# Strassen's algorithm for 18 up-projection tile pairs, with the weight sums on GpSimd

## What is computed

```python
def swiglu(x, w1, w3, w2):
    return (jax.nn.silu(x @ w1) * (x @ w3)) @ w2
...
    x = x + 0.5 * rmsnorm(swiglu(rmsnorm(x, norm_g[0]), ffn1_w1, ffn1_w3, ffn1_w2), norm_g[1])
    mo, st = mixer(rmsnorm(x, norm_g[2]), w_in, ...)
    x = x + rmsnorm(mo, norm_g[3])
    x = x + 0.5 * rmsnorm(swiglu(rmsnorm(x, norm_g[4]), ffn2_w1, ffn2_w3, ffn2_w2), norm_g[5])
```

## Time and profile before

| | us |
|---|---|
| median of 3 runs | 1088.48 |
| range of the runs | 1088.02 to 1089.86 |
| span of the profiled execution | 1087.4 |
| PE busy in it | 1077.2 (99%) |
| VectorE busy | 533.9 (49%) |
| ScalarE busy | 358.4 (33%) |
| GpSimd busy | 95.5 (9%) |

### The profile page before, as it was taken

How to read it: one execution, slowest core, us unless ns; L and a number is a source line. 1 busy time by engine, 2 the same in 40 slices (tenths; PEclk the granted TensorE clock), 3 DMA queues, 4 the chain that set the end, 5 groups by cost and what they waited for, 6 DMA issues and landing times.

```text
span 1087.4 us, 21585 instructions
## 1 busy us (share of the span) xinstructions
PE 1077.2 (99%) x8945; PEld 1063.8 (98%) x8945; DVE 533.9 (49%) x929; ACT 358.4 (33%) x527; POOL 95.5 (9%) x169
## 2 busy tenths in 40 slices
PE   8999999999999999999999999999999999999998
PEld 8999999999999999998999999999999999999997
DVE  6444524343333369685656787743323343324346
ACT  5322114222122345321537543532212222122232
POOL 0000725920000000340000000000000000000000
PEclk9999999999999999999999999999999999999999
DMA  7223232222222241123421134132222222222232
GB/s 253 83 78 96 80 94 81 93 83 91 82 88 82 78 136 40 60 78 122 135 62 59 60 117 148 40 98 95 80 94 80 94 83 91 85 90 89 76 88 83
DMA packets 30338, 99.13 MB, mean 91 GB/s; under 512 B 3652, under 2 KB 6084, under 8 KB 30152
## 3 DMA queue, kind: packets, MB, share of 16 engines
q1 hardware_dynamic: 30280, 98.33, 28.7%
HBM read 93.58 MB, written 4.74 MB: 90 GB/s over the span
## 4 chain that ended last, share of the span: by engine, by line
PE 95%; DVE 2%; ACT 1%; issue 1%; DMA 0%; SPq 0%; DVEq 0%; ACTq 0%
PE ps L2013 77%; PE ps L2038 6%; PE ps L2107 3%; PE ps L2481 2%; PE ps L2125 1%; PE ps L2045 1%; PE ps L2050 1%; PE ps L2305 0%; PE ps L2264 0%; DMA x<-xT 0%; PE ps L2255 0%; PE ps L2331 0%; DVE wl L1019 0%; PE ps L2298 0%; PE ps L2272 0%
## 5 line engine op out<-in xcount | busy, mean ns | idle before, releaser
L1019 DVE TENSOR_TENSOR wl<-raw,wh 128x1024 fp32r<-128x1024 f32 (+1 forms) x145 | 178.1, 1229 | 409.2 <-ACT wh L563 408.6
L2013 PE MATMUL ps<-xh,wh 128*128 128x272 f32 x1616 | 336.3, 289 | 1.2 <-DVE k L1437 1.0
L2013 PE MATMUL ps<-xl,wh 128*128 128x272 f32 x1616 | 333.7, 288 | 0.0
L2013 PE MATMUL ps<-xh,wl 128*128 128x272 f32 x1616 | 332.8, 287 | 0.0
L563 ACT CAST wh<-raw 128x1024 fp32r<-128x1024 f32 (+1 forms) x145 | 150.6, 1038 | 422.4 <-PE ps L2013 419.6
L2013 PEld LDWEIGHTS ps<-xh,wh 128*128 128x128 f32 x1616 | 253.0, 188 | 2.5 <-issue 1.4
L2013 PEld LDWEIGHTS ps<-xl,wh 128*128 128x128 f32 x1616 | 254.1, 189 | 0.0
L2013 PEld LDWEIGHTS ps<-xh,wl 128*128 128x128 f32 x1616 | 252.9, 188 | 0.0
L2013 PE MATMUL ps<-hh,wh 128*128 128x272 f32 x608 | 126.3, 289 | 0.5 <-DVE hl L1040 0.5
L2013 PE MATMUL ps<-hl,wh 128*128 128x272 f32 x608 | 125.4, 287 | 0.0
L2013 PE MATMUL ps<-hh,wl 128*128 128x272 f32 x608 | 125.3, 287 | 0.0
(11 more groups left out here) (483 smaller groups left out, 1181.9 us busy)
## 6 DMA issues: line engine op xcount, KB each, us to landing
raw<-w SPq DMA_DIRECT2D x118, 512.0 KB, 3.5
raw<-win SPq DMA_DIRECT2D x25, 512.0 KB, 3.5
raw<-w SPq DMA_DIRECT2D x16, 384.0 KB, 3.1
raw<-wout SPq DMA_DIRECT2D x8, 512.0 KB, 3.6
o_yT<-x SPq DMA_DIRECT2D x8, 272.0 KB, 2.2
cs<-cT SPq DMA_DIRECT2D x4, 516.0 KB, 4.4
o_sC<-cs SPq DMA_DIRECT2D x4, 516.0 KB, 6.4
x<-xT SPq DMA_DIRECT2D x3, 544.0 KB, 6.8
```

The source lines that it names most:

```text
L1019: V.tensor_tensor(wl[par][:, 0:cols], raw[par][:, 0:cols], wh[par][:, 0:cols].bitcast(F32), ALU.subtract).then_inc(split_done, 1)
L2013: last = mm(ps[:, bank + s, 0:HALF], w[:, kk * P:(kk + 1) * P], a[:, kk, s * HALF:(s + 1) * HALF], start=(kk == 0 and i == 0), stop=(kk == ...
```

## The change

18 of the 22 tile pairs (a gate tile and its up tile) of the second FFN are computed by Strassen's algorithm, in its form with seven products: the 2x2 blocks of the weights are K halves by gate and up tile (A11, A12, A21, A22), those of x are K halves by token halves. A product has 4 K tiles x 3 passes = 12 matmuls of 128x272. The four weight sums of a pair (S1 and S3 in one instruction of 1024 elements, S2 and S4 with 512 each) are made by GpSimd. The weight blocks and sums are then cast by ScalarE and get their low parts from VectorE; partial results are copied out of PSUM by ScalarE (`keep_p1`, `keep_p5`, `keep_u2`) and added in PSUM by VectorE (`c11`, `c12`, `c22`). The parts become 4, 6, 6 and 6 tiles; the first four pairs are computed as before, and a part more of eight down units comes about, with the same number of matmuls in all.

The products need a normed x. VectorE writes it (`xn`, eight instructions), GpSimd makes the four sums of its blocks (`form_t3`, `form_t24`), and ScalarE and VectorE split those and three blocks. All this stands in part 0. The results of the first four pairs are brought to the same norm by one more multiplication each (`scaled`). Loads of the pairs have buffers of their own (`pair0`, `pair1`, 1 MB a pair); the sums lie where the two `raw` buffers were.

```diff
-assert sum(PARTS) == FT
+PARTS2 = (4, 6, 6, 6)
+assert sum(PARTS) == FT and sum(PARTS2) == FT and PARTS2[-1] == PARTS[-1]
+NG = sum(PARTS2[1:])
+KH = KD // 2
+KHP = KH * P
+FORM = KH * HALF
...
+FFN2_END = FFN2_BASE + 2 * PARTS2[0] + KD * (len(PARTS2) - 1)
+EARLY_STORES = 4 + MH
...
+        pairs = [sb(f"pair{i}", [P, 4 * KHP], at=er_at + 16 * KHP * i) for i in range(2)]
+        sums = sb("sums", [P, 4 * KHP], at=raw_at)
...
+            def load_pair(j):
+                if j == 0:
+                    spe.wait_ge(out_dma, 16 * EARLY_STORES)
+                elif j == 1:
+                    spe.wait_ge(form_lo, 1)
+                else:
+                    spe.wait_ge(a22_lo, j - 1)
+                    spe.wait_ge(s4_sum, j - 1)
+                tile = 2 * (PARTS2[0] + j)
+                for c in range(2):
+                    spe.dma_start(pairs[j % 2][:, c * UNIT:(c + 1) * UNIT], A["w13_1"][tile + 1 - c]).then_inc(pair_in[j % 2], 16)
...
+                load_pair(0)
+                load_pair(1)
...
+            def hi_g(j):
+                pair_full(j)
+                if j % N6:
+                    act.wait_ge(p1_done, j)
...
+                    act.wait_ge(unit_used, down_unit(j // N6, KD - 2) + 3)
...
+            def hi_form(i, dst, src, scale):
+                act.wait_ge(form_raw, i + 1)
+                if i == 0:
+                    act.wait_ge(unit_used, FFN2_BASE + 5)
+                    act.wait_ge(out_dma, 16 * EARLY_STORES)
+                nc.scalar.activation(dst, src, ACT.Copy, scale=scale).then_inc(form_hi, 1)
...
+                silu(hb + 2, 0)
+                hi_form(0, form_hi_t[:, 2], form_t3[:], 1.0)
+                hi_form(1, form_hi_t[:, 0], xn[:, 0, 1], 1.0)
+                hi_form(2, form_hi_t[:, 1], form_t24[:], -1.0)
+                hi_form(3, form_hi_t[:, 3], form_t24[:], 1.0)
+                up_split(u0 + 7)
+                hidden_hi(hb + 2, 0, 2)
...
+                            hi_4(j)
+                            hi_a22(j)
+                            if j > j0:
+                                silu_pair(j - 1)
+                            keep_p1(j)
+                            if last:
+                                act.wait_ge(p1_done, j + 1)
+                                down(0)
+                            else:
+                                hi_g(j + 1)
+                            keep_p5(j)
+                            keep_u2(j)
+                            if last:
+                                act.wait_ge(p6_done, j + 1)
+                                down(1)
+                            else:
+                                hi_3(j + 1)
+                                hi_12(j + 1)
+                            if j > j0:
+                                hidden_hi(FT4 + j - 1, 0, j - 1 - j0)
...
+            def low(hi, j, dst, src, rounded, done):
+                dve.wait_ge(hi, j + 1)
+                V.tensor_tensor(dst, src, rounded.bitcast(F32), ALU.subtract).then_inc(done, 1)
...
+            def c22(j):
+                dve.wait_ge(p7_done, j + 1)
+                dve.wait_ge(p5_kept, j + 1)
+                a, d = bank_a(j), set_of(j) + 3
+                V.tensor_tensor(ps[:, d, 0:HALF], ps[:, a, 0:HALF], p5_keep(j), ALU.add).then_inc(c22_done, 1)
...
+                for kk in range(KD):
+                    normed(kk)
+                up_lo(u0 + 6)
+                up_first(hb + 2, 0, u0 + 4)
+                lo_form(0, form_lo_t[2][:], form_t3[:], form_hi_t[:, 2], 1.0)
+                lo_form(1, form_lo_t[0][:], xn[:, 0, 1], form_hi_t[:, 0], 1.0)
+                lo_form(2, form_lo_t[1][:], form_t24[:], form_hi_t[:, 1], -1.0)
+                scaled(hb + 2, 0)
+                lo_form(3, form_lo_t[3][:], form_t24[:], form_hi_t[:, 3], 1.0)
+                up_lo(u0 + 7)
+                gated(hb + 2, 0, u0 + 5)
+                hidden_lo(hb + 2, 0, 2)
...
+                            if j > j0:
+                                c12(j - 1)
+                            lo_4(j)
+                            lo_a22(j)
+                            c11(j)
+                            if last:
+                                down(0)
+                            else:
+                                lo_g(j + 1)
+                            if j > j0:
+                                c22(j - 1)
+                            if last:
+                                down(1)
+                            else:
+                                lo_3(j + 1)
+                                lo_12(j + 1)
+                            if j > j0:
+                                hidden(j - 1)
+                                hidden_lo(FT4 + j - 1, 0, j - 1 - j0)
...
+            pool.wait_ge(xn_ready, KD)
+            pool.wait_ge(out_dma, 16 * EARLY_STORES)
+            G.tensor_tensor(form_t3[:], xn[:, 1, 1], xn[:, 0, 1], ALU.subtract).then_inc(form_raw, 1)
+            pool.wait_ge(form_raw, 1)
+            G.tensor_tensor(xn[:, 0, 1], xn[:, 0, 0], xn[:, 0, 1], ALU.subtract).then_inc(form_raw, 1)
+            pool.wait_ge(form_raw, 2)
+            G.tensor_tensor(form_t24[:], xn[:, 0, 1], xn[:, 1, 1], ALU.add).then_inc(form_raw, 1)
+            pool.wait_ge(form_lo, 3)
+            G.tensor_tensor(form_t24[:], form_t24[:], xn[:, 1, 0], ALU.subtract).then_inc(form_raw, 1)
+            for j in range(NG):
+                w = pairs[j % 2]
+                pool.wait_ge(pair_in[j % 2], 32 * (j // 2 + 1))
+                if j % N6:
+                    pool.wait_ge(s12_lo, j)
+                    pool.wait_ge(s3_lo, j)
+                else:
+                    pool.wait_ge(split_done, down_unit(j // N6, KD - 1) + 3)
+                if j:
+                    pool.wait_ge(s4_sum, j)
+                G.tensor_tensor(two(sums[:, 2 * KHP:]), two(w[:, KHP:3 * KHP]),
+                                w[:, A21B].unsqueeze(1).to_broadcast([P, 2, KHP]), ALU.add).then_inc(s13_sum, 1)
+                pool.wait_ge(s13_sum, j + 1)
+                G.tensor_tensor(sums[:, S2B], sums[:, S1B], w[:, A11B], ALU.add).then_inc(s2_sum, 1)
+                if j:
+                    pool.wait_ge(s4_lo, j)
+                pool.wait_ge(s2_sum, j + 1)
+                G.tensor_tensor(sums[:, S4B], sums[:, S2B], w[:, A12B], ALU.add).then_inc(s4_sum, 1)
...
+            def product(w, at, form, bank, first, done=None):
+                (w_hi, w_lo), (f_hi, f_lo) = w, form
+                for kk in range(KH):
+                    cut = slice(at + kk * P, at + (kk + 1) * P)
+                    for i, (a, f) in enumerate(((w_hi, f_hi), (w_hi, f_lo), (w_lo, f_hi))):
+                        ins = mm(ps[:, bank, 0:HALF], a[:, cut], f[:, kk], start=(first and kk == 0 and i == 0),
+                                 stop=(kk == KH - 1 and i == 2), skip_group_check=True)
+                if done is not None:
+                    ins.then_inc(done, 1)
...
+            def p4(j):
+                pe.wait_ge(a22_lo, j + 1)
+                pe.wait_ge(c22_done, j + 1)
+                product(a22_w[j % 2], 0, form_x[3], bank_a(j), False, p4_done)
...
+                            p2(j)
+                            p1(j)
+                            if j > j0:
+                                p7(j - 1)
+                            p5(j)
+                            p6(j)
+                            if j > j0:
+                                p4(j - 1)
+                            p3(j)
+                        p7(j)
+                        enter_down(0)
+                        down(0, range(0, 3))
+                        p4(j)
+                        down(0, range(3, n - 1))
+                        enter_down(1)
+                        down(1, range(0, n - 1))
+                        down(0, range(n - 1, n))
+                        down(1, range(n - 1, n))
...
-                if b == 1:
+                if b > 0:
```

348 lines of the change are left out of this document (339 added, 9 removed).

## The result

| | before | after |
|---|---|---|
| median of the runs, us | 1089.06 (1088.02 to 1089.86, 4 runs) | 1104.41 (1101.29 to 1107.65, 4 runs) |
| ratio, 95% interval | | 1.0139 [1.0116, 1.0162] |
| span of the profiled execution, us | 1087.4 | 1105.8 |
| mean granted clock of that span | 1.000 | 0.988 |
| first matmul of the mixer's last entry unit to first half unit of FFN 2, us | 364.7 | 382.4 |

The kernel became slower by 15.3 us (1.4%). The forecast was 7.3 us slower, so the direction was right and the size was half of what came. The last row of the table is the stretch in which everything that changed lies. It grew by 17.7 us in the profiled executions (after's is the slowest of its four runs, 1107.65); ahead of it the unchanged code came 0.9 us later by chance, and the tail behind it stayed the same (32.0 us before, 31.8 after).

The account below looks back on a forecast made before the run. PE's matmuls were taken to bound the kernel: 27.1 us removed, 33.2 us of waits added where 0.5 were before, net +5.6, plus 1.7 for the clock and 1.1 from span to median, gave 1095.8 us from 1087.4; range 1081.0 to 1106.0.

Parts of the forecast that it names:

- Removed work: 18 tile pairs of the second FFN: 84 matmuls each instead of 96, 27.1 us less.
- (a): Unit 6 of part 0: PE waits 2.2 us for its low part, behind VectorE's writing of xn.
- (f): Inside the parts: c22 comes 0.8 us late in two of each part's pairs, as GpSimd holds VectorE; 4.7 us.
- (b): Unit 7: PE waits 11.5 us for its low part, behind four low parts of forms and GpSimd's sums.
- (c): Down unit 2 of part 0: waits 1.6 us for y's first evacuation, and 0.1 before it.
- (d): Down unit 2 of parts 1 to 3: weights free late, then cast and low part; 1.95 each, 5.9 us.
- (e): First and second pairs of a part: products wait for [A11 A12] and sums; 2.2 and 5.0 us.
- Exclusion in one lane: In the pairs: VectorE instructions with two SBUF inputs and GpSimd sums exclude each other, filling 9.7 of 10.5 us.
- (g): Granted clock after PE's 11 us stand at unit 7: 1.7 us lost, at least nothing, at most twice that.
- The lane costs little: Rival for the pairs: GpSimd's sums let VectorE in or run some 20% faster; 1082.6 us, chance 0.20.
- The lane overflows: Rival for the pairs: longer sums or slower loads, c22 late in nearly every pair; 1103 us, chance 0.15.
- The prologue alone: Rival for part 0: the wait at unit 7 is shorter, 1088 +- 1, no change; near nothing, chance 0.10.

Follow-up runs that it names:

- e10_all_vector: After with activation blocks spread out, second pair's load moved, down unit 0 finished early, c22 placed earlier, pairs' weight sums on VectorE; 1075.27 us, 0.9867 of before.
- e3_small_sums: After with GpSimd's weight sums cut to 8 columns, casts and low parts reading raw blocks; 1089.57 us.
- e5_free_sums: After with GpSimd's weight sums at full size, but casts and low parts reading raw blocks and no cast waiting for a sum; 1102.67 us.
- e11_all_gpsimd: After with blocks spread out, load moved, down unit 0 finished early, c22 earlier, weight sums left on GpSimd; 1081.34 us, 0.9916 of before.
- e1_fill: After with filler matmuls, whose results nobody reads, put on TensorE ahead of nine of its waits; 1099.72 us.
- e9_prologue3: After with the seven activation blocks spread out and the second pair's load queued behind down unit 3's; 1092.82 us.
- e12_stands: The kernel before with five TensorE stands of some 2.0 us put into its second FFN; 1103.56 us, 1.0124 of before.

## Why the prediction was right in direction and half in size

- **Removed work, 27.1 us.** Right. It comes out once the waits go: e10_all_vector's stretch is 14.8 us shorter than before's, with 8.8 us of holes of 0.4 us and more and one short fall of the clock (1.6 us) in it; the other 1.9 are in gaps too small to be told apart.
- **Waits (a) to (f), 33.2 us.** Right place by place, 35.2 us in all: (a) 2.42 against 2.2, (b) 11.41 against 11.5, (c) 1.74 against 1.7, (d) 6.2 against 5.9, (e) 7.9 against 7.2, (f) 5.5 against 4.7. All but (b) are a little longer than laid out, 2.0 us together.
- **Exclusion in one lane.** Right, and shown by e3_small_sums against e5_free_sums. The lengths taken from two short rows held: 2.4 us for 1024 columns where 2.37 was taken. The reason given for (f), that c22 is late because the lane is full, was only half of it: c22 had a better place free, and with it e11_all_gpsimd has no such wait under the same sums.
- **(g) The clock, 1.7 us, 3.4 at most.** This is the step that failed. It asked only what a stand of 11 us costs and took the cold start for it; unit 7 then took 8.16 us instead of 6.02, 2.1 us, within its bounds. But the layout itself held seven more stands of 2 us, and the step gave them nothing, without a reason. Four of them were followed by a fall, 1.6 us each. In the profiled executions the clock cost 8.0 us (the stretch of e1_fill against after's) to 9.6 (with the 1.6 us that e1_fill's filler ran over its stands), so some 7 us more than forecast. Over the medians it is 4.7 to 6.3, so 3 to 4.6 more. Together with the 2.0 us of longer waits that is 5.0 to 6.6 of the 8.6 us between 1095.8 and 1104.4. The kernel before was itself 0.6 us slower beside after than in the runs the forecast started from. Some 1.4 to 3 us of the medians remain open. The profiled executions close better: holes 35.2, clock 2.1 + 4 x 1.6 = 8.5, less 27.1, are 16.6 of the 17.7 us by which the stretch grew, and the rest is of the size of e10_all_vector's small gaps.
- **The rivals.** "The lane costs little" fell on the means of 1978 and 1360 ns. "The lane overflows" gave 1103 and was nearest in time, but for a cause that isn't there: c22 is late in seven places, not in nearly all, and from the second pair of a part on the pairs start 10.6 to 11.6 us apart, with 12.1 only in the two where the clock fell. "The prologue alone" fell with (b), which measured 11.41 us.
- **What would show it.** The single wait of 9 to 12 us near 720 to 732, the clock below 1.00 behind it, the raised means and the waits on L1438 all came. The sign that would have shown the failed step, falls of the clock elsewhere, was not on the list.
- **Small slips in the sums.** The ten durations of VectorE's pair add up to 7.2 us, and to 6.4 with the overlap that is named beside them, not to 7.1; 6 x 0.8 in (f) is 4.8, not 4.7. Neither moves the forecast by more than 0.1 us.
- **What was left open.** How the sums would stand on VectorE, no run showed then: with c22 in its place they made the kernel 6.1 us faster than on GpSimd (1075.27 against 1081.34), the order ahead of a part's first pair included.

## What to carry to other kernels

A forecast that finds many small stands of TensorE has to price the clock behind each of them too, not only behind the longest: here 2 us of waiting came to 3.6 whenever the clock fell. Before a difference of some us between two kernels is put down to an edit, count the falls in both profiles: e9_prologue3 got 6 of its 14.6 us from falls that happened not to come. Before a queue is called full, ask which operation in it somebody waits for, and whether it stands behind ones that nobody waits for; the same work in another order turned +15 us into -8 with the same engines and into -14 with the sums on VectorE. And when a wait is removed, look at every queue that it had covered, the transfers' among them: twice here the next one in line took most of it.

## What the runs showed of the hardware

- The granted clock fell to its lower level (0.50) behind stands of TensorE of 2.05 to 2.16 us, for about 3.4 us, 1.6 us lost each time; in after behind four of seven stands of 2.05 to 2.42 us, in e12_stands behind one of five, over all profiled executions behind 30 of 64 of 2.0 to 2.6 us and behind none of 16 of 1.2 to 1.8 us. Filler matmuls in the stands' place kept it at 1.00.
- A GpSimd sum of 1024 columns took 2.39 to 2.41 us undisturbed, of 512 columns 1.28 to 1.30. One of 768 columns that reads the same tile for both inputs took 1.47, all five times, less than the 1.8 that an estimate from the others gives (1.29 for 512 and 2.40 for 1024); why, no run tells.
- GpSimd sums that no cast waits for cost 13 us over 18 pairs (e5_free_sums against e3_small_sums), by holding VectorE's instructions with two SBUF inputs; VectorE's additions in PSUM kept their 0.44 us.
